# Attention units of two tiles issued in pairs, and expert ids decoded for two heads at once

## What is computed

```python
w = softmax(logits)[0] - lam * softmax(logits)[1]        # differential attention, per head
sv, si = top_k(s, 16)                                    # two lists per head
top_s, top_p = top_k(sv[0][:, None] + sv[1][None, :], 16)
idx = si[0][top_p >> 4] * 128 + si[1][top_p & 15]        # the expert ids
a   = sum(x * u_tab[idx]);  out = sum(softmax(top_s) * gelu(a) * v_tab[idx])
```

## Time and profile before

| | |
|---|---|
| median of three runs | 3188.34 us (3184.56 to 3188.40) |
| profiled execution | 3192.09 us, its span 3190.1 us |
| mean granted clock of TensorE | 0.874 of full speed |
| busy, PE / DVE / ACT / POOL | 2449.7 / 2259.8 / 1989.4 / 1221.5 us |
| moved by DMA | 1256.05 MB, 1040 of it gathers of 1 MB |
| mean DMA rate | 394 GB/s |

### The profile page before, as it was taken

How to read it: one execution, slowest core, us unless ns; L and a number is a source line. 1 busy time by engine, 2 the same in 40 slices (tenths; PEclk the granted TensorE clock), 3 DMA queues, 4 the chain that set the end, 5 groups by cost and what they waited for, 6 DMA issues and landing times.

```text
span 3190.1 us, 42742 instructions
## 1 busy us (share of the span) xinstructions
PE 2449.7 (77%) x13752; PEld 2024.4 (63%) x13752; DVE 2259.8 (71%) x5825; ACT 1989.4 (62%) x3694; POOL 1221.5 (38%) x1095
## 2 busy tenths in 40 slices
PE   8886878766978777886877687888787565587777
PEld 6555767655777666775765566776576555546665
DVE  2625678886467877778856877677668888678655
ACT  1325567797566865556655796555656666657883
POOL 1113333434444443343434344334444444444341
PEclk9878989887989889898888898998799877877899
DMA  7558999989999999999999999999999999999996
GB/s 291 185 215 354 397 418 406 401 364 405 411 419 420 421 420 421 421 420 416 383 420 421 382 421 421 421 420 421 418 419 420 405 422 420 414 375 421 421 421 278
DMA packets 182544, 1256.05 MB, mean 394 GB/s; under 512 B 21359, under 2 KB 26223, under 8 KB 33585
## 3 DMA queue, kind: packets, MB, share of 16 engines
q0 software_dynamic: 156320, 1113.83, 84.9%
q1 hardware_dynamic: 24416, 136.35, 10.7%
q10 hardware_dynamic: 1584, 3.15, 0.3%
HBM read 1246.78 MB, written 6.50 MB: 393 GB/s over the span
## 4 chain that ended last, share of the span: by engine, by line
DMA 37%; PE 25%; DVE 17%; ACT 11%; issue 4%; DVEq 3%; ACTq 2%; POOL 1%; SPq 0%; POOLq 0%
DMA arena<-in_uv,idx 35%; DVE arena L1672 9%; PE acc L1919 8%; PE bank L1946 6%; ACT arena L1180 5%; PE bank L1937 4%; PE bank L1718 2%; PE bank L1752 1%; DMA panel<-in_panels 1%; POOL arena L989 1%; DVEq L1578 1%; ACT act_w L1169 1%; ACT L1166 1%; ACTq L1167 1%; ACT L1159 1%
## 5 line engine op out<-in xcount | busy, mean ns | idle before, releaser
L989 POOL DMA_INDIRECT arena<-in_uv,idx x1024 | 1176.1, 1149 | 1724.2 <-PE acc L1919 1496.9
L1919 PE MATMUL acc<-cst,arena 128*128 128x128 f32 x8128 | 1245.7, 315 | 631.5 <-ACT arena L1180 630.8
L1919 PEld LDWEIGHTS acc<-cst,arena 128*128 128x128 f32 x8128 | 1094.2, 163 | 804.2 <-ACT arena L1180 777.4
L1672 DVE CUSTOM_DVE_ANT_0 arena<-arena,h 128x1024 f32<-128x1024 f32 x1024 | 1230.3, 1222 | 491.5 <-DMA arena<-in_uv,idx 484.0
L1180 ACT ACTIVATE arena<-arena,act_w 128x1024 f32<-128x1024 f32 x1016 | 1112.0, 1141 | 37.0 <-issue 2.4
L1166 ACT ACTIVATE act_w<-dots 128x2 f32<-128x2 f32 x520 | 105.3, 203 | 840.0 <-DVE dots L1672 839.0
L1946 PE MATMUL bank<-hT,panel 128*128 128x264 f32 (+2 forms) x1856 | 431.5, 389 | 6.5 <-issue 6.5
L1946 PEld LDWEIGHTS bank<-hT,panel 128*128 128x128 f32 x1856 | 352.4, 201 | 58.4 <-issue 8.9
L1169 ACT ACTIVATE act_w<-act_w 128x1 f32<-128x1 f32 x1040 | 249.5, 286 | 44.3 <-issue 2.2
L1166 ACT ACT_TABLE_LOAD x111 | 142.4, 1283 | 1.6
L1718 PE MATMUL bank<-hT,panel 128*128 128x264 f32 (+1 forms) x512 | 120.7, 397 | 19.1 <-DMA panel<-in_panels 13.6
(11 more groups left out here) (241 smaller groups left out, 2262.2 us busy)
## 6 DMA issues: line engine op xcount, KB each, us to landing
panel<-in_panels SPq DMA_DIRECT2D x116, 1024.0 KB, 9.3
arena<-in_uv,idx POOLq DMA_INDIRECT x1024, 19.9
arena<-in_cache_k POOLq DMA_DIRECT2D x16, 512.0 KB, 6.6
arena<-in_cache_v POOLq DMA_DIRECT2D x16, 512.0 KB, 4.8
arena<-out_y_s POOLq DMA_DIRECT2D x8, 512.0 KB, 9.0
arena<-in_panels SPq DMA_DIRECT2D x4, 1024.0 KB, 8.2
h<-in_h SPq DMA_DIRECT2D x2, 1024.0 KB
out_y_p<-h SPq DMA_DIRECT2D x3, 512.0 KB
```

The lines of the kernel that those rows point to most:

```text
L989: nc.gpsimd.indirect_dma_start(uv[:, slot_of(e), :], None, uv_dram[layer], bass.IndirectOffsetOnAxis(ids[:, r:r + 1], 0)).then_inc(gathere ...
L1672: V.tensor_tensor_reduce(uv[:, slot_of(e), 0:D], uv[:, slot_of(e), 0:D], x_rows, 1.0, 0.0, ALU.mult, ALU.add, dots[:, G % 2, r:r + 1]).the ...
L1919: m = mm(acc[:, c * P:(c + 1) * P], uv[:, slot_of(e), D + c * P:D + (c + 1) * P], const("ident"), is_transpose=True, start=False, stop=Tru ...
```

## The change

There are two edits. The first puts both units of a pair of heads into one lot for `score` and `weigh`, and their `w_turn` and `pv` into lots that follow each other. Tile 2's units stood at lots 36, 39, 43, 46, 50, 53, 57, 60 and stand in pairs at 36, 43, 50, 57; tile 3's stood at 64, 66, ... 78 and stand in pairs at 64, 68, 72, 76.

```diff
-            for b, at in ((2, 36 + 7 * (j // 2) + 3 * (j % 2)), (3, 64 + 2 * j)):
+            for b, at in ((2, 36 + 7 * (j // 2)), (3, 64 + 4 * (j // 2))):
                 u = b * HEADS + j
                 lots[at] += self.score[u]
                 lots[at + 1].append(self.weigh[u])
-                lots[at + 4].append(self.w_turn[u])
-                lots[at + 7].append(self.pv[u])
+                lots[at + 4 + j % 2].append(self.w_turn[u])
+                lots[at + 7 + j % 2].append(self.pv[u])
```

```diff
-                V.max_index(r_ti[:, 8:16], r_tv[:, 8:16], r_wk)
-                dve.drain()
-                V.tensor_scalar(r_ij[:, 0:16], r_ti, 4, None, ALU.logical_shift_right)
-                V.tensor_scalar(r_ij[:, 16:32], r_ti, 15, None, ALU.bitwise_and)
-                dve.drain()
-                V.tensor_copy(r_ijf, r_ij)
+                V.max_index(r_ti[:, unit % 2, 8:16], r_tv[:, 8:16], r_wk)
...
+            def route_ids(b, hd, sets):
+                n = sets.stop - sets.start
...
+                V.tensor_scalar(ij[:, :, 0, :], r_ti[:, sets, :], 4, None, ALU.logical_shift_right)
+                V.tensor_scalar(ij[:, :, 1, :], r_ti[:, sets, :], 15, None, ALU.bitwise_and)
+                dve.drain()
+                V.tensor_copy(ijf, ij)
+                dve.drain()
...
-                V.scalar_tensor_tensor(out=idx[:, b, hd, :], in0=r_e[:, 0:16], scalar=float(KEYS), in1=r_e[:, 16:32],
-                                       op0=ALU.mult, op1=ALU.add).then_inc(idx_done, 1)
+                V.scalar_tensor_tensor(out=idx[:, b, hd + 1 - n:hd + 1, :], in0=e[:, :, 0, :], scalar=float(KEYS), in1=e[:, :, 1, :],
+                                       op0=ALU.mult, op1=ALU.add).then_inc(idx_done, n)
...
-                        route_ids(x.b, x.hd)
                         if not place(x.layer, x.b):
+                            route_ids(x.b, x.hd, slice(x.u % 2, x.u % 2 + 1))
                             gates(x.b, x.hd, x.u)
-                        elif x.hd == HEADS - 1:
+                        elif x.hd % 2 == 1:
+                            route_ids(x.b, x.hd, slice(0, 2))
+                        if place(x.layer, x.b) and x.hd == HEADS - 1:
```

More of the change, by code:

```diff
@@ L695, in build @@
         r_wk = yb[:, 256:512]
-        r_eq = yb[:, 512:1024]
+        r_eq = yb
         r_cand = ya[:, 0:256]
@@ L699, in build @@
         r_si = ya[:, 288:320].bitcast(U32)
-        r_sif = ya[:, 320:352]
+        r_sif = ya[:, 548:612].rearrange("p (a n) -> p a n", a=2)
         r_tvs = [ya[:, 352:368], ya[:, 514:530]]
[L702 to L705, removed]
+        r_ti = ya[:, 320:352].rearrange("p (a n) -> p a n", a=2).bitcast(U32)
+        r_ij = ya[:, 0:64].rearrange("p (a c k) -> p a c k", a=2, c=2).bitcast(U32)
+        r_ijf = ya[:, 64:128].rearrange("p (a c k) -> p a c k", a=2, c=2)
+        r_e = ya[:, 128:192].rearrange("p (a c k) -> p a c k", a=2, c=2)
         r_nms = [ya[:, 480:481], ya[:, 481:482]]
@@ L1526, in route_pairs @@
                 dve.drain()
-                V.tensor_copy(r_sif, r_si)
+                V.tensor_copy(r_sif[:, unit % 2, :], r_si)
                 V.max(r_tv[:, 0:8], r_cand)
@@ L1534, in route_top @@
                 dve.drain()
-                V.max_index(r_ti[:, 0:8], r_tv[:, 0:8], r_cand)
+                V.max_index(r_ti[:, unit % 2, 0:8], r_tv[:, 0:8], r_cand)
                 V.match_replace(r_wk, r_tv[:, 0:8], r_cand, LOWEST)
@@ L1545, in route_top @@
                 dve.drain()
-                V.tensor_copy(r_ijf, r_ij)
-            def route_ids(b, hd):
+                V.tensor_copy(ijf, ij)
                 dve.drain()
-                V.tensor_tensor(r_eq.rearrange("p (k i) -> p k i", i=16),
-                                r_ijf.rearrange("p (k i) -> p k i", i=1).broadcast_to([P, 32, 16]),
-                                const("iota").rearrange("p (k i) -> p k i", k=1).broadcast_to([P, 32, 16]),
+                eq = r_eq[:, 512 * sets.start:512 * sets.stop]
@@ L1554, in route_ids @@
+                V.tensor_tensor(eq.rearrange("p (k i) -> p k i", i=16),
+                                ijf.rearrange("p a c (k i) -> p (a c k) i", i=1).broadcast_to([P, 32 * n, 16]),
+                                const("iota").rearrange("p (k i) -> p k i", k=1).broadcast_to([P, 32 * n, 16]),
                                 ALU.is_equal)
                 dve.drain()
-                eq4 = r_eq.rearrange("p (c k i) -> p c k i", c=2, i=16)
-                V.tensor_tensor(eq4, eq4, r_sif.rearrange("p (c k i) -> p c k i", c=2, k=1).broadcast_to([P, 2, 16, 16]),
-                                ALU.mult)
+                eq4 = eq.rearrange("p (c k i) -> p c k i", c=2 * n, i=16)
@@ L1559, in route_ids @@
+                V.tensor_tensor(eq4, eq4, r_sif[:, sets, :].rearrange("p a (c k i) -> p (a c) k i", c=2, k=1)
+                                .broadcast_to([P, 2 * n, 16, 16]), ALU.mult)
                 dve.drain()
-                V.tensor_reduce(r_e, r_eq.rearrange("p (k i) -> p k i", i=16), AX_X, ALU.add)
+                V.tensor_reduce(e.rearrange("p a c k -> p (a c k)"), eq.rearrange("p (k i) -> p k i", i=16), AX_X, ALU.add)
                 dve.drain()
-                V.scalar_tensor_tensor(out=idx[:, b, hd, :], in0=r_e[:, 0:16], scalar=float(KEYS), in1=r_e[:, 16:32],
-                                       op0=ALU.mult, op1=ALU.add).then_inc(idx_done, 1)
+                V.scalar_tensor_tensor(out=idx[:, b, hd + 1 - n:hd + 1, :], in0=e[:, :, 0, :], scalar=float(KEYS), in1=e[:, :, 1, :],
+                                       op0=ALU.mult, op1=ALU.add).then_inc(idx_done, n)
```

1 line of the change is left out of this document (added).

## The result

The changed kernel takes 3195.9 us as a median of 13 runs; the kernel before, beside it, 3187.4 us as a median of 13. The ratio is 1.0025, 95% interval 1.0016 to 1.0034: slower by 8 us (5 to 11). The time lies inside the range of 3174 to 3197, but the change went the other way, on the side that got 0.19.

The account below looks back on a forecast made before the run. DMA was taken to bound most of the run, ScalarE tile 3 by 2.3 us a pair. Tile 3 -1.0, tile 2 0 and second edit -1.5 made -2.5 us: 3185.8 against a median of 3188.3, range 3174 to 3197.

Parts of the forecast that it names:

- upper bound of +6.4: Tile 3: the case that TensorE works slower behind standstills, making the chain 3.7 us longer at lots 72 and 76.
- Lot 72, the chain: Tile 3's pair at 72: TensorE, VectorE and ScalarE wait in turn behind a `pv` reading; 25.0 us against 23.6.
- Lot 76: Tile 3's pair at lot 76: by the same count as at lot 72, 22.5 us instead of 22.3.
- Lot 64: Tile 3's first pair: 1.8 us shorter, since a `w_turn` and a table switch leave the tile's start.
- Tile 2: Pairs in tile 2: loads not the bound, waits shorter than the gathers in flight; 0, bounds -3 and +7 us.
- (c): Bank wait at lots 50, 57, 72, 76: a score waits for ScalarE to read a `pv`; 3 to 5 us each.
- Second edit: Ids of two heads decoded by one wider instruction set, 40 to 54 us less VectorE; -1.5 us, bounds -5 and +3.
- dips are shallow: DMA dips at 1500 to 1560 and 1780 to 1840 us: less recoverable than their rate tells; -1.5 us taken.
- late ids: Last tile: even heads' ids come with the odd one's; 3.7 us if uncovered, 0.13 together with no effect.
- "Slower": Rival: slots come free one lot later at lots 50, 57, 72, 76, costing 20 less 10.3: 3198 us; chance 0.18.
- "Faster": Rival: waits find ScalarE busy anyway, all tile 3's loads are recovered, -10.3 us: 3175 us; chance 0.27.
- (a): Tile 3, lots 68, 72, 76: VectorE's logits wait for the preceding pair's odd `w_turn`; no size of its own.

Follow-up runs that it names:

- f1: Changed kernel with the pairs' `w_turn` 3 and 4 lots behind the scores instead of 4 and 5: 3191.8 us, ratio 1.0009 to the kernel before.
- f3: Changed kernel with `w_turn` 3 and 4 and `pv` 5 and 6 lots behind the scores: 3185.0 us, ratio 0.9988 to the kernel before.
- f2: Changed kernel with the pairs' `pv` 6 and 7 lots behind the scores instead of 7 and 8: 3190.8 us, ratio 0.9999 to the kernel before.
- g1: Changed kernel with two heads' ids decoded by two narrow instruction sets once the odd head is done: 3202.2 us, ratio 1.0044 to the kernel before.
- e4: Kernel before with tile 2's units alone in pairs, ids decoded head by head: 3195.5 us, ratio 1.0022.
- h3: Changed kernel profiled again with nothing altered, the last of three such repeats: 3196.1 us.
- e2: Kernel before with the second edit alone, units where they stood: 3187.9 us, ratio 0.9995.
- g2: Changed kernel with tile 3's pairs five lots apart, `pv` 6 and 7 lots behind scores, tile 2 as in f3: 3179.9 us, ratio 0.9983 to before.

## Why the prediction was wrong

**What failed** is one step: "Sum: +1.4 - 0.8 + 0.2 - 1.8 = -1.0 us" for tile 3, the time that the waits of a pair cost ScalarE against the loads that it saves. The mechanism, a pair that waits for the pair before it, was named rightly; its price was set too low. Lots 64 to 96 took 7.4 us more, beyond the upper bound of +6.4, and DMA moved 338 GB/s from 640 to 740, where the forecast had a little more than 365. By ends of ScalarE's scalings, as means of the four executions less the two of before, the pairs cost:

```
pair at (ScalarE from, to)    forecast    measured
64      (lot 63 to 69)          -1.8        +1.8
68      (69 to 73)              -0.8        +0.3
72      (73 to 77)              +1.4        +3.0
76      (77 to 81)              +0.2        +3.0
```

- **Lot 72, the chain.** Counted at 25.0 us against 23.6; measured 25.4 against 23.6, where TensorE kept its higher level. VectorE's logits were due 4.9 us behind ScalarE's last scaling and came at 5.1 (691.57 to 696.70). The working was right to 0.4 us where the granted clock behind the wait was 1.00; what was mis-sized is TensorE at its lower level behind the wait, which I kept as a bound only and which came in three executions of four, with 1.6 us.
- **Lot 76.** It has the same two waits, and the count there gave them little more than the two loads saved (22.5 against 22.3 us). It took 25.4. VectorE waited 5.5 us for the turn, the longest of the three. Of f1 to f3, those without the bank wait have these four lots at 21.1 (f2) and 21.6 us (f3); f1, which keeps it, has 24.7. So the bank wait and what follows from it, not the burst, are the price here.
- **Lot 64.** The load and the turn that leave the tile's start were to save 1.8. ScalarE did less, but GpSimd's longest wait grew from 10.5 to 13.4 us, and from 640 to 740 VectorE waited 3.9 us for gathers, where it waited 1.8 before; ScalarE's lots 68 and 69 ended 5.2 and 5.0 us behind the one before, near DMA's pace (two of 2.50). So a count of ScalarE's own time may not hold behind a stall that empties the ring. That is argued from the trace: no run took this stall away alone, and other forms with a pair at 64 take 33.4 (f1) to 37.6 us (g1) here, against 33.1 and 33.9 before. The cause of this +1.8 stays open.

The parts of the miss, measured less forecast, are 3.6, 1.1, 1.6 and 2.8 us from top to bottom.

**Tile 2.** Forecast 0, bounds -3 and +7; +2.6 in the traces, +7 alone (e4). Ahead of 640 us two waits (c) came, 4.6 us together and the longest 3.8 (5.6 in h3). In tile 3 they were not the 3 to 5 us that were forecast for each lot: at 72 and 76 no single one was over 2.4.

**Second edit.** Alone -1.6 us by time, as forecast (-1.5), which is in part luck: behind lot 96 it was worth about 5.5 us in the traces, at the edge of the bound of -5, and beside pairs 7 to 12 us by time, beyond it. So by its own sign the prediction was wrong here too: it named itself wrong if time came or went elsewhere than 500 to 740, and 5.0 us went behind lot 96. The argument that dips are shallow failed at 1780 to 1840: VectorE was busy 52.7 us instead of 55.6 and DMA moved 406 instead of 369 GB/s, and in e2, without pairs, 52.7 and 399. At 1500 to 1560 DMA moved 381 instead of 363. The late ids held GpSimd for 5.7 us, where the forecast had 3.7, and most of it was hidden by the gathers in flight, as forecast: the rest behind lot 512 is +0.7.

**The rivals.** "Slower", bank wait (c), had the right head of the chain and the wrong size for it: 20 us for four whole lots, of which about 12 us came for both waits together (f3 against the changed kernel). Its condition, more than half of each wait reaching DMA, seems met in tile 3, by single profiles: with the bank wait gone (f2) lots 64 to 96 take 187.8 us, 6.2 below the changed kernel's mean, of the 10 counted for lots 72 and 76. "Faster" asked for all loads of tile 3 to be recovered, 10.3 us. ScalarE was relieved of 9.8 us in lots 64 to 81, and these lots as a whole were not shortened by it in any form, in g2 and f3 either. So the reading that ScalarE is the bound in tile 3 by 2.3 us a pair is not borne out by any run. Without waits (a) and (c) both edits together are worth 5 us (g2), not 13, and the second edit can account for all of it.

## What to carry to other kernels

Two units put into one step save two table loads, but they also bring the second unit's buffers due one step earlier: before pairing, list for every buffer in a ring of two or four which reader frees it, and where that reader now stands in its own engine's stream. Where there are several waits in one chain, removing its head (here the bank) shortens the others too, and removing a later one moves the wait forward. A busy share of 96% does not show that an engine's own work is the bound: time taken from it may come back as waits. When runs differ by more than the effect, cut single profiles into stretches between marks of one queue, and take several of each kernel: in the stretch that mattered the two executions of before were 0.3 us apart, but the four of the changed kernel 5.0.

## What the runs showed of the hardware

- TensorE, at the same place of the same program, takes 1.91 us for 16 matmuls in one execution, at a granted clock of 1.00, and 3.50 in another, at 0.54, behind waits of 1.29 and 1.40 us. The Trainium skill (TensorE: Matmul & The Clock Gate, What's actually happening) says that the number of slow matmuls at a kernel's start varies from run to run of one kernel; these executions show the same in the middle of one. By the two levels, 2.4 and 1.2 GHz, 1.91 us would be 3.8 if all 16 were at the lower. So a wait has a tail that a single profile may not show.
- Two executions of the kernel before issued their first gather at 219.3 and 210.1 us, and were within 0.9 us of each other from there to the end. Their spans differ by 8.3 us, so the start explains the difference.
